# The compression of the sparse attention writes to PSUM banks 4 and 5 instead of 0 and 1

## The chip, the cores and the metric

The kernel runs on one core of a Trainium2 chip. The metric is the device time of one execution in microseconds (us), the median over the runs shown. Traces come from a profiled execution of the same program.

## The reference, cut to what matters

The kernel takes x (512 positions by 1024 channels, fp32) through four layers. The first two (a block with dilated attention and a gated convolution, then one with retention, each with a conv-GLU feed-forward) lie ahead of the place that the change touches. The last two are alike: a hybrid mixer and a feed-forward, each with a norm before and after. The mixer's input projection gives, among others, queries for 8 sparse-attention heads and keys and values for 2 KV heads in three kinds: compressed, selected, windowed. The part that matters here is the compression:

```
blocks = k[:, idx] + pe                      # 31 blocks of 32 positions, stride 16
flat   = blocks as rows of 32*64
kc, vc = gelu(flat @ w1 + b1) @ w2           # for keys (i = 0) and values (i = 1)
```

The keys go through a rotary embedding first ("rope"), the values do not.

## The kernel before

**Layout.** Activations lie transposed: 128 channels on the partitions, 512 positions along the free dimension. Every fp32 matmul with a weight is made as three fp32r matmuls, high times high (L496), low weight times high (L499) and high times low (L503). ScalarE makes the high part of each weight piece from the ring of four 512 KB slots (L1016), VectorE the low part (L1397); SyncE loads the ring, one unit behind the other.

**PSUM banks.** There are eight. `next_bank()` deals them in rotation from a list, and one counter (`turn[1]`) runs through the whole program. In the input projection of a hybrid layer the list is `[0, 1, 4, 5, 6, 7]`; banks 2 and 3 serve the norm. `empty(b)` makes TensorE wait until the last reader of bank b has told its semaphore, as the table `vacated` has it.

**The order on TensorE in hybrid layer l (0 or 1).** Five tiles of the projection are made together (`group`, tiles g 0 to g 4, five banks of the rotation), then tiles 5, 6 and 7 one after the other (three more banks). Then comes the compression (L863 to L883): for i = 0 and 1 and two parts each, 16 x 2 matmuls of 64x64 weights with 32 columns (L879), 64 columns of one bank for each i. It waits for the rope of tile g 0 (i = 0) or for tile g 1 read out (i = 1), for the bank, and for each raw weight unit. Behind it comes `by_token(("tm", l))` (L573, L574, L577): four banks, 0 to 3, in turn, 8 weight pieces, 280 columns; inside it, after the fourth piece, the second matmuls of the compression (`compressed`, L893 and L897), into banks 4, 5 and 6.

**The readers.** VectorE reads the eight tiles of the projection out, times the norm's row (`times_rs`, L1447), in the order g 0, g 1, g 2, and then, for r = 2 to 6:

```
        for r in range(2, 7):
            key = ("n", l, "g", r + 1) if r < 4 else ("n", l, r + 1)
            lo_for(("n", l, 5))
            rope(r - 2)
            lo_for(("n", l, 6))
            q.wait_ge(F.dve, ("rope", l, r - 2))
            times_rs(K.tmp(2 * r % 4), key, s, ("ra", l, r))
```

So tile 5 is read out only after `rope(2)`, tile 6 after `rope(3)` and tile 7 after `rope(4)`. A rope swaps halves by four small DMAs (`half_turn`, L431, on SyncE's queue, among the loads of the ring, L453), multiplies the swapped copy on VectorE (L1839) and the straight one on GpSimd (L2054), and adds the two (L1842). The swap of rope(r) starts when its tile has been read out; the copies share two buffers by turns.

ScalarE copies the compression's bank to SBUF (`hb`, L1298), VectorE adds the parts up (L1862 to L1865) behind its last `times_rs`, and ScalarE makes the gelu (L1302). Between the two i, ScalarE and VectorE make the first three `tm` weight pieces; they lie behind `hb(0)` and behind VectorE's sums for i = 0 in their engines' order.

Of the kernel before, what the change touches and what calls it, by code (L numbers as in the profile page):

```python
# [13 lines left out]
ACT = mybir.ActivationFunctionType  # L14
# [376 lines left out]
def build(nc, D, out):  # L391
    with ExitStack() as ctx:
        K = memory(nc, ctx)
        K.D, K.out, K.W = D, out, weights(D)
        for program in (sync_program, scalar_program, vector_program, gpsimd_program, tensor_program):
            program(Count(), Queue(None), K)
        for flag in K.F:
            flag.count = 0
        block = ctx.enter_context(nc.Block())

        @block.sync
        def _(e):
            sync_program(e, Queue(e), K)

        @block.scalar
        def _(e):
            scalar_program(e, Queue(e), K)

        @block.vector
        def _(e):  # L410
            vector_program(e, Queue(e), K)

        @block.gpsimd
        def _(e):
            gpsimd_program(e, Queue(e), K)

        @block.tensor
        def _(e):
            tensor_program(e, Queue(e), K)
# [49 lines left out]
def tensor_program(e, q, K):  # L469
    F, W, BK = K.F, K.W, K.BK  # L470
    vacated = {}
# [3 lines left out]
    def empty(b):  # L475
        for flag, event in vacated.get(b, ()):
            q.wait_ge(flag, event)
# [248 lines left out]
    for i in range(NQ):  # L726
        m = e.transpose(BK[4][0:48, i * 128:(i + 1) * 128], K.HL[:, 48 * i:48 * i + 48].bitcast(F32), K.cs("ident"))
# [4 lines left out]
    for n, j in enumerate((0, 4, 1, 5, 2, 6, 3, 7)):  # L732
# [6 lines left out]
        m = e.matmul(BK[b][:, :], K.wh(p, c * 128, 128), K.RT, start=True, stop=True)  # L739
# [71 lines left out]
    for h in range(4):  # L811
        for kt in range(NQ):
            w = S - kt * 128
            empty(kt)
            for part in range(2):
                for which in range(2):
                    q.wait_ge(F.pool, ("rot", h, which, part))
                m = e.matmul(BK[kt][:, 0:w], K.RQ[2 + part][:, kt * 128:(kt + 1) * 128], K.RQ[part][:, kt * 128:S],
                             start=part == 0, stop=part == 1)
# [4 lines left out]
        for m_ in range(4):  # L824
            empty(m_)
            for kt in range(NQ):
                q.wait_ge(F.dve, ("wt", h, kt))
                q.wait_ge(F.dve, ("rvc", h, kt))
                m = e.matmul(BK[m_][:, kt * 128:S], K.RV[:, kt * S + m_ * 128:kt * S + (m_ + 1) * 128],  # L829
                             K.WT[kt][:, 0:S - kt * 128], start=kt == 0, stop=kt == 3, skip_group_check=True)  # L830
# [25 lines left out]
    for l in range(2):  # L856
# [8 lines left out]
        for i in range(2):  # L865
            c = (K.kcr, K.vcr)[i]
            if i == 0:
                q.wait_ge(F.dve, ("rope", l, 0))
            else:
                q.wait_ge(F.dve, ("freed", "n", l, "g", 1))  # L870
            q.wait_ge(F.dve, ("pe", l))
            empty(i)
            for part in range(2):
                u = W.raws["w1", l, 2 * i + part]
                q.wait_ge(K.landed(u), ("unit", u))
                for n in range(16):
                    for kv in range(2):
                        r = slice(64 * kv, 64 * kv + 64)
                        m = e.matmul(BK[i][r, 32 * part:32 * part + 32], K.slot(u)[r, n * 64:(n + 1) * 64],  # L879
                                     c[r, 2 * part:2 * part + 32, n], start=part == 0 and n == 0, stop=n == 15,  # L880
                                     skip_group_check=True)
                m.then_inc(F.attn.tell(("cmp", l, i, part), ("unit", u)), 1)
            vacated[i] = [(F.act, ("hb", l, i))]  # L883

        def compressed():

# [17 lines left out]
        for g in range(4):  # L904
# [4 lines left out]
            for i in range(NQ):  # L909
                c0 = (g % 2 * 4 + i) * 64  # L910
                m = e.matmul(BK[b][:, c0:c0 + 64], K.NQT[g][:, i * 128:(i + 1) * 128], K.kcc, start=True, stop=True,
                             skip_group_check=True)
# [87 lines left out]
def scalar_program(e, q, K):  # L1000
    F, W, BK = K.F, K.W, K.BK
    nxt = [0]

    def hi_to(p):

        while nxt[0] <= min(p, len(W.pieces) - 1):
            i = nxt[0]
            nxt[0] += 1
            u, c, w = W.pieces[i]
            if i == 0:  # L1010
                q.wait_ge(F.first, "first")
            else:
                q.wait_ge(K.landed(u), ("unit", u))
            if i >= SPLIT:
                q.wait_ge(F.proj, ("piece", i - SPLIT))
            e.activation(K.wh(i, 0, w), K.raw(i), ACT.Copy, bias=0.0, scale=1.0).then_inc(F.hi.tell(("piece", i)), 1)  # L1016
# [271 lines left out]
    for l in range(2):  # L1288
# [6 lines left out]
            hi_for(("n", l, i))  # L1295
        for i in range(2):
            q.wait_ge(F.attn, ("cmp", l, i, 1))
            e.activation(K.hb(i), BK[i][:, 0:64], ACT.Copy, bias=0.0, scale=1.0).then_inc(F.act.tell(("hb", l, i)), 1)  # L1298
            if i == 0:
                hi_to(W.first["tm", l] + 2)  # L1300
            q.wait_ge(F.dve, ("hid", l, i))
            e.activation(K.hid[:, 64 + 32 * i:95 + 32 * i], K.hid[:, 32 * i:32 * i + 31], ACT.Gelu_apprx_tanh,  # L1302
                         bias=K.SM[:, 160 + i:161 + i], scale=1.0).then_inc(F.act.tell(("gel", l, i)), 1)
# [32 lines left out]
        for t in range(18):  # L1336
            pair = (2 * t, 2 * t + 1)
            kt = 3 - t % 4
            if t < 16:
                if t and (t - 1) % 4 < 3:  # L1340
                    for n in (2 * t - 2, 2 * t - 1):
                        m, kt1 = n // 8 * 2 + n % 2, 3 - n % 8 // 2
# [895 lines left out]
```

## Time and profile before

| what | value |
|---|---|
| runs before (us) | 3029.17, 3024.3, 3022.35; median 3024.3 |
| the profiled execution's own time | 3025.72 us |
| its span | 3024.0 us |
| mean granted TensorE clock | 0.994 |
| TensorE busy | 2997.6 us (99%) |
| VectorE, ScalarE, GpSimd busy | 1770.5, 1268.6, 151.0 us |

The busy time of an engine is that of its instructions; a granted clock of 1.00 is 2.4 GHz, 0.50 is 1.2 GHz. A timeline row has the start, the time taken, the engine, the line, and in brackets the idle time ahead with the work that ended it. PEld is TensorE's weight load.

### The profile page before, as it was taken

The numbers are of one execution on the slowest core, as the hardware profiler recorded it, in microseconds if no ns is written. First come the engines' busy times: TensorE is split into PE (matmuls) and PEld (weight loads), VectorE is DVE, ScalarE is ACT, GpSimd is POOL, SyncE is SP. The second block draws the span as 40 slices with busy tenths as digits, with TensorE's granted clock in tenths as the row PEclk, the third lists the DMA queues.
The fourth block names the chain that finished last, engine by engine and source line by source line (L and its number), as shares of the span: only waits on it lengthen the run. The fifth ranks groups of instructions, "written<-read, shape, count | busy, mean of one in ns | idle before, by whom it ended". The sixth has DMA issues, their size and how long they took to land.

```text
span 3024.0 us, 37960 instructions
## 1 busy us (share of the span) xinstructions
PE 2997.6 (99%) x14676; PEld 2403.7 (79%) x14676; DVE 1770.5 (59%) x3129; ACT 1268.6 (42%) x2377; POOL 151.0 (5%) x203
## 2 busy tenths in 40 slices
PE   9999999999999999999999999999999999999998
PEld 7778888878888888888876687888887766888887
DVE  4666775345555587634565558774455655587743
ACT  4444443322333344432366535443233655354431
POOL 0100000000000000001001101000020011010000
PEclk9999999999999999999999999999989999999999
DMA  4222322222222333334201132322242111223332
GB/s 150 76 98 91 102 96 96 97 77 84 84 77 85 97 98 98 98 96 133 91 29 49 42 98 84 105 97 95 80 125 90 33 46 46 94 85 104 98 98 70
DMA packets 74724, 263.97 MB, mean 87 GB/s; under 512 B 9008, under 2 KB 9008, under 8 KB 74416
## 3 DMA queue, kind: packets, MB, share of 16 engines
q1 hardware_dynamic: 73680, 258.13, 26.4%
q10 hardware_dynamic: 864, 3.41, 0.3%
q8 instruction: 116, 1.90, 0.3%
q14 instruction: 64, 0.52, 0.1%
HBM read 255.74 MB, written 2.10 MB: 85 GB/s over the span
## 4 chain that ended last, share of the span: by engine, by line
PE 89%; DVE 7%; ACT 2%; issue 1%; DMA 1%; POOL 0%; SPq 0%; DVEq 0%; POOLq 0%; ACTq 0%
PE bank L496 24%; PE bank L503 23%; PE bank L499 23%; PE bank L573 2%; PE bank L577 2%; PE bank L574 2%; PE bank L661 2%; PE bank L693 2%; PE bank L675 1%; DVE wl L1397 1%; PE bank L829 1%; PE bank L930 1%; DVE x L1821 1%; DVE big L1981 1%; PE bank L960 1%
## 5 line engine op out<-in xcount | busy, mean ns | idle before, releaser
L1397 DVE TENSOR_TENSOR wl<-ring,wh 128x512 fp32r<-128x512 f32 (+1 forms) x946 | 650.8, 694 | 824.9 <-ACT wh L1016 819.9
L496 PE MATMUL bank<-xh,wh 128*128 128x512 f32 x2464 | 982.1, 399 | 3.3 <-ACT xh L1023 2.6
L499 PE MATMUL bank<-xh,wl 128*128 128x512 f32 x2464 | 961.9, 390 | 2.3 <-DVE wl L1397 2.3
L503 PE MATMUL bank<-xl,wh 128*128 128x512 f32 x2464 | 924.0, 390 | 0.0
L1016 ACT ACTIVATE wh<-ring 128x512 fp32r<-128x512 f32 (+1 forms) x946 | 580.4, 622 | 788.6 <-PE bank L503 706.0
L496 PEld LDWEIGHTS bank<-xh,wh 128*128 128x128 f32 x2464 | 463.5, 188 | 137.3 <-issue 37.0
L503 PEld LDWEIGHTS bank<-xl,wh 128*128 128x128 f32 x2464 | 463.0, 188 | 98.6 <-DVE xl L1490 0.4
L499 PEld LDWEIGHTS bank<-xh,wl 128*128 128x128 f32 x2464 | 463.7, 188 | 93.3 <-DVE wl L1397 4.8
L496 PE MATMUL bank<-bigr,wh 128*128 128x512 f32 x1024 | 399.0, 390 | 0.5 <-ACT bigr L1380 0.5
L499 PE MATMUL bank<-bigr,wl 128*128 128x512 f32 x1024 | 398.4, 389 | 0.0
L503 PE MATMUL bank<-bigr,wh 128*128 128x512 f32 x1024 | 393.4, 389 | 0.0
L496 PEld LDWEIGHTS bank<-bigr,wh 128*128 128x128 f32 x1024 | 192.2, 188 | 41.3 <-ACT bigr L1380 1.4
L503 PEld LDWEIGHTS bank<-bigr,wh 128*128 128x128 f32 x1024 | 192.2, 188 | 40.8 <-DVE bigr L1985 0.9
L499 PEld LDWEIGHTS bank<-bigr,wl 128*128 128x128 f32 x1024 | 192.2, 188 | 39.7
L1193 ACT ACTIVATE tmp<-tmp,vec 128x512 f32<-128x512 f32 x136 | 104.7, 770 | 182.0 <-DVE tmp L1447 182.0
L1085 ACT ACTIVATE pp<-pp,sm 128x512 f32<-128x512 f32 (+3 forms) x160 | 88.3, 553 | 90.6 <-DVE sm L1466 90.5
L1203 ACT ACTIVATE bigr<-tmp 128x512 fp32r<-128x512 f32 x88 | 55.6, 632 | 138.3 <-DVE tmp L1654 138.3
L2010 POOL TENSOR_TENSOR sm<-sm,cst 128x4 f32<-128x4 f32 x16 | 16.6, 1037 | 1936.1 <-DVE sm L1419 1601.9
L1447 DVE TENSOR_TENSOR big<-bank,rs 128x512 f32<-128x512 f32 x106 | 71.6, 687 | 68.6 <-PE bank L503 65.4
L1447 DVE TENSOR_TENSOR tmp<-bank,rs 128x512 f32<-128x512 f32 x154 | 105.3, 684 | 6.0 <-ACT rs L1031 4.3
L573 PE MATMUL bank<-wh,xh 128*128 128x512 f32 (+1 forms) x288 | 107.9, 375 | 0.0
L577 PE MATMUL bank<-wl,xh 128*128 128x512 f32 (+1 forms) x288 | 106.7, 370 | 0.1
(204 smaller groups left out, 2777.6 us busy)
## 6 DMA issues: line engine op xcount, KB each, us to landing
ring<-in_w_up SPq DMA_DIRECT2D x176, 512.0 KB, 3.4
ring<-in_w_down SPq DMA_DIRECT2D x88, 512.0 KB, 3.4
ring<-in_w_in SPq DMA_DIRECT2D x64, 512.0 KB, 3.5
ring<-in_w_ret SPq DMA_DIRECT2D x32, 512.0 KB, 3.2
ring<-in_w_even SPq DMA_DIRECT2D x19, 512.0 KB, 3.3
ring<-in_w_ret_v SPq DMA_DIRECT2D x16, 512.0 KB, 3.2
ring<-in_w_ret_out SPq DMA_DIRECT2D x16, 512.0 KB, 3.3
ring<-in_w_proj SPq DMA_DIRECT2D x16, 512.0 KB, 3.5
```

Of the source, the lines that this page charges most:

```text
L496: e.matmul(o, K.wh(p, c * 128, 128), oh, start=start, stop=False, skip_group_check=True)
L499: e.matmul(o, K.wl(p, c * 128, 128), oh, start=False, stop=False, skip_group_check=True)
L503: m = e.matmul(o, K.wh(p, c * 128, 128), ol, start=False, stop=stop, skip_group_check=True)
L573: e.matmul(o, K.XH[:, c], K.wh(p, 0, n), start=k == 0, stop=False)
L574: e.matmul(o, K.XL[:, c], K.wh(p, 0, n), start=False, stop=False)
L577: m = e.matmul(o, K.XH[:, c], K.wl(p, 0, n), start=False, stop=k == DT - 1)
L661: m = e.matmul(BK[i][:, u.at:u.at + w], u.q[r, u.qt * 128:w], u.k[r, 0:w], start=True, stop=True, skip_group_check=True)
L1016: e.activation(K.wh(i, 0, w), K.raw(i), ACT.Copy, bias=0.0, scale=1.0).then_inc(F.hi.tell(("piece", i)), 1)
L1085: e.activation(p, p, ACT.Exp, bias=K.den(t, 2 * part + i, 0), scale=-1.0, accum_out=K.den(t, 2 * part + i, 1)).then_inc(F.act.tell(("exp", ...
L1193: e.activation(K.tmp((2 * i + 1) % 5), K.up(i), ACT.Identity, bias=b, scale=w[2]).then_inc(F.act.tell(("tap", f, i)), 1)
L1397: e.tensor_tensor(K.wl(i, 0, w), K.raw(i), K.wh(i, 0, w).bitcast(F32), ALU.subtract).then_inc(F.lo.tell(("piece", i)), 1)
L1447: e.tensor_tensor(dst, K.bank(key)[:, :], K.RSB[:, :], ALU.mult).then_inc(F.dve.tell(("freed", *key), *events), 1)
```

## The change

The compression writes to banks 4 + i instead of i, it waits for those banks to be empty, `vacated` has the entry for them, and ScalarE's copy reads from them. Nothing else differs.

```diff
@@ -869,18 +869,18 @@
             q.wait_ge(F.dve, ("pe", l))
-            empty(i)
+            empty(4 + i)
             for part in range(2):
                 u = W.raws["w1", l, 2 * i + part]
                 q.wait_ge(K.landed(u), ("unit", u))
                 for n in range(16):
                     for kv in range(2):
                         r = slice(64 * kv, 64 * kv + 64)
-                        m = e.matmul(BK[i][r, 32 * part:32 * part + 32], K.slot(u)[r, n * 64:(n + 1) * 64],
+                        m = e.matmul(BK[4 + i][r, 32 * part:32 * part + 32], K.slot(u)[r, n * 64:(n + 1) * 64],
                                      c[r, 2 * part:2 * part + 32, n], start=part == 0 and n == 0, stop=n == 15,
                                      skip_group_check=True)
                 m.then_inc(F.attn.tell(("cmp", l, i, part), ("unit", u)), 1)
-            vacated[i] = [(F.act, ("hb", l, i))]
+            vacated[4 + i] = [(F.act, ("hb", l, i))]
@@ -1295,7 +1295,7 @@
             q.wait_ge(F.attn, ("cmp", l, i, 1))
-            e.activation(K.hb(i), BK[i][:, 0:64], ACT.Copy, bias=0.0, scale=1.0).then_inc(F.act.tell(("hb", l, i)), 1)
+            e.activation(K.hb(i), BK[4 + i][:, 0:64], ACT.Copy, bias=0.0, scale=1.0).then_inc(F.act.tell(("hb", l, i)), 1)
```

## Rows read from the trace of the kernel before

**Rows 1.** The page: engines busy, and the chain that ended last by engine.

```profile
PE 2997.6 (99%) x14676; PEld 2403.7 (79%) x14676; DVE 1770.5 (59%) x3129; ACT 1268.6 (42%) x2377; POOL 151.0 (5%) x203
PE 89%; DVE 7%; ACT 2%; issue 1%; DMA 1%; POOL 0%; SPq 0%; DVEq 0%; POOLq 0%; ACTq 0%
```

**Rows 2.** Timeline of TensorE, layer 1: last projection matmul, compression, by-token matmuls.

```profile
2231.62 0.39 PE L503 MATMUL bank<-xl,wh 128*128 128x512 f32 x1
2235.46 4.78 PE L879 MATMUL bank<-big,ring 64*64 64x32 f32 x97 [3.45 <-DVE tmp L1447]
...
2248.67 0.60 PE L573 MATMUL bank<-wh,xh 128*128 128x280 f32 x1
...
2249.30 0.43 PE L577 MATMUL bank<-wl,xh 128*128 128x280 f32 x1
2249.53 0.43 PE L573 MATMUL bank<-wh,xh 128*128 128x280 f32 x1
```

**Rows 3.** Timeline of VectorE, layer 1: tiles 5 and 7 read out, and what follows.

```profile
2234.67 0.69 DVE L1447 TENSOR_TENSOR tmp<-bank,rs 128x512 f32<-128x512 f32 x1
...
2240.19 0.69 DVE L1839 TENSOR_TENSOR pp<-pp,rope 128x512 f32<-128x512 f32 x1 [1.25 <-DMA pp<-tmp]
...
2242.84 0.69 DVE L1447 TENSOR_TENSOR tmp<-bank,rs 128x512 f32<-128x512 f32 x1
...
2243.81 1.17 DVE L1397 TENSOR_TENSOR wl<-ring,wh 128x280 fp32r<-128x280 f32 x3
```

**Rows 4.** Timeline of SyncE's DMA issues, layer 1: two swaps and the loads behind.

```profile
2231.29 2.40 SPq L431 DMA_DIRECT2D pp<-tmp  x4
...
2235.39 3.37 SPq L431 DMA_DIRECT2D pp<-tmp  x4
2238.80 6.88 SPq L453 DMA_DIRECT2D ring<-in_w_tm  x3
```

**Rows 5.** Stretches, layers 1 and 0: length, busy PE, PEld, DVE, ACT, POOL, clock, DMA.

```profile
2236.00:2236.50 0.50, 0.50 (x20) 0.50 (x18) 0.29 (x1) 0.00 (x0) 0.50 (x1) 0.72 0.90 369
...
2244.00:2249.00 5.00, 5.00 (x90) 4.93 (x89) 0.97 (x3) 0.47 (x2) 0.00 (x0) 0.50 0.47 136
...
2253.00:2253.50 0.50, 0.50 (x5) 0.50 (x4) 0.50 (x1) 0.00 (x0) 0.50 (x1) 0.72 1.02 418
...
1413.00:1417.00 4.00, 4.00 (x132) 3.79 (x130) 1.02 (x3) 0.00 (x0) 1.71 (x1) 1.00 0.70 198
```

**Rows 6.** Timeline of TensorE, layer 0: compression, then by-token matmuls.

```profile
1413.22 7.66 PE L879 MATMUL bank<-big,ring 64*64 64x32 f32 x256
1420.81 0.40 PE L573 MATMUL bank<-wh,xh 128*128 128x280 f32 x1
...
1422.02 0.29 PE L574 MATMUL bank<-wh,xl 128*128 128x280 f32 x1
1422.15 0.29 PE L577 MATMUL bank<-wl,xh 128*128 128x280 f32 x1
```

**Rows 7.** Timeline of VectorE, layer 0: tiles 5 and 6 read out.

```profile
1412.44 0.69 DVE L1447 TENSOR_TENSOR tmp<-bank,rs 128x512 f32<-128x512 f32 x1
...
1417.53 0.69 DVE L1447 TENSOR_TENSOR tmp<-bank,rs 128x512 f32<-128x512 f32 x1
```

**Rows 8.** Timeline of ScalarE, layer 0: the compression's banks copied out.

```profile
1417.19 0.22 ACT L1298 ACTIVATE big<-bank 128x64 f32<-128x64 f32 x1 [14.11 <-PE bank L879]
...
1421.54 0.20 ACT L1298 ACTIVATE big<-bank 128x64 f32<-128x64 f32 x1
```

**Rows 9.** Timeline of the weight loads, layer 0: what the by-token matmuls waited for.

```profile
1421.40 0.19 PEld L577 LDWEIGHTS bank<-wl,xh 128*128 128x128 f32 x1 [0.30 <-DVE wl L1397]
1421.79 0.19 PEld L573 LDWEIGHTS bank<-wh,xh 128*128 128x128 f32 x1 [0.20 <-ACT big L1298]
```

**Rows 10.** An idle stretch of over 1 us elsewhere: timeline, and the stretch around it.

```profile
95.24 0.50 PE L739 MATMUL bank<-bigr,wh 128*128 128x512 f32 x1 [1.18 <-DVE big L1557]
...
95.00:100.00 5.00, 4.11 (x10) 1.70 (x11) 5.00 (x9) 1.09 (x1) 0.00 (x0) 1.00 0.32 105
```

## The prediction

> **What bounds the kernel.** I read the page first: TensorE is busy for 2997.6 of 3024.0 us and carries 89% of the chain that ended last [rows 1]. A microsecond in which TensorE stands still in the middle is thus a microsecond of the total, unless a later wait on something other than TensorE takes it up. Next I read the timeline of TensorE around line 879, once in each hybrid layer. In layer 1 the projection ends at 2231.62 + 0.39 = 2232.01 and the compression starts at 2235.46, after an idle stretch of 3.45 us; it is let go by a VectorE read-out [rows 2]. That is the one starting 2234.67 and ending 2235.36 [rows 3]. In layer 0 there is no such gap [rows 6]. Then the stretches: in layer 1 the granted clock falls to half during the half microsecond from 2236.0 and comes back in the one from 2253.0; in layer 0 it stays 1.00 [rows 5]. 256 matmul records of compression thus take 2248.67 - 2235.46 = 13.21 us in layer 1 [rows 2] and 1420.81 - 1413.22 = 7.59 us in layer 0 [rows 6].
>
> **Who held the banks.** The question is who was last in banks 4 and 5. The counter of the rotation has to be counted in the code. Ahead of layer 0 it has dealt 5 + 12 + 8 banks in the first block, 52 in each feed-forward (5 + 39 + 8) and 16 + 12 + 8 in the retention: 25 + 52 + 36 + 52 = 165, which is 3 modulo 6. Layer 0 therefore gives tiles g 0 to g 4 the banks 5, 6, 7, 0, 1 and tiles 5, 6, 7 the banks 4, 5, 6. One layer deals 8 + 8 + 16 + 4 + 16 + 8 + 52 = 112, 4 modulo 6. Layer 1 starts one place in: g 0 to g 4 in 1, 4, 5, 6, 7, and tiles 5, 6, 7 in 0, 1, 4. The trace bears this out: in layer 1 bank 0 would be freed by tile 5, the read-out at 2234.67, and that is the one TensorE waited for. So the new waits are: layer 0, i = 0 for tile 5 and i = 1 for tile 6; layer 1, i = 0 for tile 7, and i = 1 for tile g 2, long read out.
>
> **The change, layer 1.** Tile 7's read-out starts at 2242.84 and ends at 2243.53 [rows 3]; TensorE followed such an end by 0.10 us (2235.46 against 2235.36), so the compression starts at 2243.63. Is that end itself moved? It hangs on rope(4): tile 5 read out at 2235.36, its swap issued at 2235.39 [rows 4], landed for VectorE's multiply at 2240.19, then GpSimd's product, the sum, and the read-out at 2242.84 [rows 3]. No step waits for the compression; the ring load queued behind the swap on SyncE (2238.80) waits for it, the swap does not [rows 4]. At best the swap gains from there being no `tm` load beside it and issues in 2.40 us like the one before, instead of 3.37 [rows 4]: 0.97 us sooner. At worst nothing is gained. I take nothing, because the `tm` load starts only after the swap's last issue, and keep 1.0 us for the range. **Start: + 2243.63 - 2235.46 = + 8.17 us**, idle 3.45 + 8.17 = 11.6 us.
>
> How fast does it then run? Before, the first 0.76 us ran at the full clock (2235.46 to about 2236.22, from the mean of 0.72 in its half microsecond) and did 0.76 / 7.59 x 256 = 26 records; the other 230 took 12.45 us. All 256 at half clock are 12.45 x 256 / 230 = 13.86 us. The clock fell 4.2 us after the last projection matmul; 11.6 us of idling holds that, so all of it runs at half. **+ 0.65 us.** The clock did not come back in 12.45 us of compression, but 2253.3 - 2248.67 = 4.6 us into the by-token matmuls; I take the same again (0). The bound there: a by-token matmul takes its turn every 0.13 us at the full clock [rows 6] and every 0.23 us at half clock [rows 2], so if the clock rose 2 us sooner or later it moves the time by about 1 us either way.
>
> The records have 32 columns. The Trainium skill ("TensorE: Matmul & The Clock Gate", section "Wait — 56ns, not 53.3ns?") states a floor of about 25 ns start to start however few the columns, and columns over 1.2 GHz when cold, 26.7 ns here: by it the compression would take as long at one clock as at the other, and the 0.65 would be nothing, the sum 8.9. The rows speak against it for this pair of small weight load and matmul: 7.59 / 256 = 30 ns and 13.86 / 256 = 54 ns. The rows decide.
>
> **The change, layer 0.** For i = 0, tile 5 is read out at 1412.44 + 0.69 = 1413.13 [rows 7], plus 0.10 is 1413.23, and the compression started at 1413.22 [rows 6]: 0, at most 0.1. For i = 1, the first half ends near 1417.02 (ScalarE's copy starts at 1417.19 [rows 8], half of 7.59 us past the start is 1417.02). Tile 6 is read out at 1417.53 + 0.69 = 1418.22 [rows 7], start 1418.32: TensorE stands 1.30 us. What is taken away: by_token waited 0.30 us for the low piece, and then 0.20 us for `hb(1)` ahead of its second bank [rows 9]. Its first matmul starts at 1420.81 [rows 6], its fourth at 1421.79 [rows 9]. Now the first starts at 1422.11. The low piece was ready by 1421.40 (the L577 start [rows 9]), hb(1) is no longer asked for, so the fourth follows after 0.23 (the step behind a restart, 1421.79 to 1422.02) + 0.13 + 0.13 (the step after it [rows 6]) = 0.49 us, at 1422.60. **+ 0.81 us.** What loses its cover: ScalarE's copy of i = 1 moves from 1421.54 to about 1422.2, and with it gelu and weight pieces 3 and 4; TensorE needs piece 3 only after 36 matmuls of 0.13 us, at 1426.8, so nothing shows. The third `tm` load waits for the first part of i = 1 and comes 1.3 us later, for pieces 6 and 7; also covered. VectorE queues nothing new behind TensorE: in layer 0 its wait for hb(0) ends as before.
>
> In layer 1 the loads of all three `tm` units, ScalarE's copies and VectorE's sums slide by the same 8.2 us as TensorE, with the same leads or, at half clock, longer ones: 0.
>
> **Sum.** 8.17 + 0.65 + 0.81 = 9.6 us. Nothing behind takes it up: TensorE is idle for 3024.0 - 2997.6 = 26.4 us in all [rows 1], of which 3.45 is the wait that grows here, and no load runs short that a pause would let catch up. Against the profiled execution (3025.72, span 3024.0) it gives 3035.3; against the median of the runs shown, 1.4 below it, 3033.9. I give 3034.
>
> **Rivals.**
> 1. *The clock also falls in layer 0.* The new 1.3 us idle lies in the midst of the sparse compression matmuls. For it: in layer 1 the clock fell after 3.45 us of idling although the compression had been running again for 0.76 us, so such work counts for little. Against: 7.6 us of it kept the clock in layer 0 [rows 5], and an idle of 1.18 us elsewhere left the clock up, though it lay among dense work [rows 10]. Price: up to 3.8 us of compression at 54 instead of 30 ns, 3.1 us, and 4.6 us of by-token matmuls at 0.23 instead of 0.13 us, 2.0 us; from half of each to all of it 2.6 to 5.1 more, 3036.6 to 3039.1. The Trainium skill, same page, section "A second HAM failure mode: psum-queue depth-cycling", says that brief idles between groups while banks are cycled make the clock go to and fro; it would bring this rival about, and no row decides it. Chance 0.2.
> 2. *Not slower: bank 4 is free early in layer 1.* If my count is off and bank 4 was last a g tile, the wait of 3.45 us goes instead of growing. It decides at 2232.01: a holder read out by then costs nothing. TensorE then starts at 2232.1 and finishes at the full clock at 2239.7, but by_token needs the low piece that VectorE makes at 2243.81, behind tile 7's read-out [rows 3]; it starts near 2244.3 in place of 2248.67, 4.4 us sooner, and 2 more if the clock holds. With layer 0's 0.8 that is 3020.7, down to 3018.7. Against it: the count, and that the wait in the trace fits it. Chance 0.04.
> 3. *Most of it is not seen.* The fall of the clock in layer 1 of the profiled execution was close (a gap of 3.45 us). Should the other executions of before differ from it, or the swap go much faster unhindered, the difference is smaller: start + 7.2, rise of the clock 2 us sooner, 1 us off; with layer 0 it is about 7, and with the spread of the runs (3022.35 to 3029.17) it may read below 6. About 3030. Chance 0.12. If on the contrary some executions of before kept the clock, theirs lay lower and the new one always pays: that end is 3039 to 3040.
>
> **How the numbers follow.** Forecast 0.64, rivals 0.2, 0.04, 0.12. The range runs from 3030 (rival 3, the 1.0 us of the swap, the spread of the runs) to 3040 (rival 1 at its dearest). About 0.2%, 6 us, is what a measurement of this kernel can tell from no change: forecast and rival 1 lie beyond it, rival 3 within it, rival 2 within or below. Faster 0.03, same 0.12, slower 0.85.
>
> **What would show it.** In layer 1, idle before line 879 of some 11.6 us ended by the VectorE read-out that follows the last rope; a granted clock of 0.50 that starts in that idle stretch and lasts till 4 or 5 us into the by-token matmuls, and 13.9 us of compression. In layer 0, an idle of 1.3 us in mid-compression, the L577 and L573 waits gone, and 1.00 throughout. Wrong would be: a wait ended by another tile's read-out, no idle in layer 1, or a later stage in which TensorE waits less than before.

## The result, and the profile after

| | before | changed |
|---|---|---|
| median of 7 runs each (us) | 3024.73 | 3032.05 |
| lowest to highest | 3022.35 to 3029.17 | 3029.9 to 3037.51 |
| span of the profiled execution | 3024.0 | 3029.6 |
| its own time | 3025.72 | 3031.38 |

The ratio is 1.0027, with a 95% interval from 1.0016 to 1.0039: 7.3 us slower by the medians, where 9.6 were forecast. A second set of runs, made later (below), gave 3034.52 against 3025.88, a ratio of 1.0025 (1.0015 to 1.0034).

Timeline of TensorE in the changed kernel, layer 1, the rows that answer to [rows 2]:

```profile
2230.29 0.39 PE L503 MATMUL bank<-xl,wh 128*128 128x512 f32 x1
2241.32 13.86 PE L879 MATMUL bank<-big,ring 64*64 64x32 f32 x256 [10.64 <-DVE tmp L1447]
2255.11 0.60 PE L573 MATMUL bank<-wh,xh 128*128 128x280 f32 x1
```

The idle stretch has grown from 3.45 to 10.64 us, and it is again a VectorE read-out that ends it. Which one shows in VectorE's timeline of the same stretch, which answers to [rows 3]:

```profile
2233.33 0.69 DVE L1447 TENSOR_TENSOR tmp<-bank,rs 128x512 f32<-128x512 f32 x1
...
2236.65 0.69 DVE L1447 TENSOR_TENSOR tmp<-bank,rs 128x512 f32<-128x512 f32 x1
2237.88 0.69 DVE L1839 TENSOR_TENSOR pp<-pp,rope 128x512 f32<-128x512 f32 x1 [0.54 <-DMA pp<-tmp]
2239.80 0.69 DVE L1842 TENSOR_TENSOR big<-tmp,pp 128x512 f32<-128x512 f32 x1 [1.22 <-POOL tmp L2054]
2240.52 0.69 DVE L1447 TENSOR_TENSOR tmp<-bank,rs 128x512 f32<-128x512 f32 x1
```

The three read-outs are those of tiles 5, 6 and 7. The last ends at 2241.21 and TensorE follows at 2241.32: bank 4 was tile 7's. It starts 7.19 us behind tile 5's here, and 8.17 before. The difference begins in the swap of the last rope. From its first issue on SyncE's queue (SPq) to the multiply on VectorE that waits for it, it took 3.83 us here (2234.05 to 2237.88) and 4.80 before; the four issues took 2.41 us, and 3.37 in [rows 4]:

```profile
2234.05 2.41 SPq L431 DMA_DIRECT2D pp<-tmp  x4
2244.97 7.16 SPq L453 DMA_DIRECT2D ring<-in_w_tm  x3
```

The stretches (columns as in [rows 5]: length, busy time of PE, PEld, DVE, ACT and POOL, granted clock, DMA share, GB/s):

```profile
2231.00:2234.00 3.00, 0.00 (x0) 0.00 (x0) 1.75 (x3) 0.00 (x0) 1.50 (x1) 1.00 0.78 261
2234.00:2241.00 7.00, 0.00 (x0) 0.00 (x0) 3.94 (x7) 0.00 (x0) 3.40 (x2) 0.50 0.30 97
2241.00:2255.00 14.00, 13.69 (x256) 13.72 (x256) 1.71 (x7) 1.41 (x5) 0.00 (x0) 0.50 0.33 98
2255.00:2257.50 2.50, 2.50 (x14) 2.44 (x13) 1.55 (x7) 0.87 (x3) 1.28 (x1) 0.50 0.43 105
2257.50:2258.50 1.00, 1.00 (x8) 1.00 (x7) 0.23 (x1) 0.29 (x1) 0.00 (x0) 0.79 0.33 70
1411.00:1419.00 8.00, 7.94 (x258) 7.62 (x256) 3.95 (x7) 1.54 (x5) 3.42 (x2) 1.00 0.68 219
```

The clock falls in the idle stretch, stays at half through the whole compression (2241.32 to 2255.11, 13.79 us) and rises about 2.8 us into the by-token matmuls (a mean of 0.79 in the microsecond from 2257.5 puts it near 2257.9). In layer 0 it stays up. Layer 0 on TensorE, first its weight loads and then its matmuls, to be read with [rows 6] and [rows 9]:

```profile
1411.20 3.83 PEld L879 LDWEIGHTS bank<-big,ring 64*64 64x64 f32 x128 [0.35 <-DVE tmp L1447]
1415.21 3.81 PEld L879 LDWEIGHTS bank<-big,ring 64*64 64x64 f32 x128 [0.18 <-DVE tmp L1447]
1420.09 0.19 PEld L577 LDWEIGHTS bank<-wl,xh 128*128 128x128 f32 x1 [0.73 <-DVE wl L1397]
```

```profile
1411.22 7.92 PE L879 MATMUL bank<-big,ring 64*64 64x32 f32 x256
1419.07 0.40 PE L573 MATMUL bank<-wh,xh 128*128 128x280 f32 x1
1419.30 0.29 PE L574 MATMUL bank<-wh,xl 128*128 128x280 f32 x1
1420.09 0.40 PE L577 MATMUL bank<-wl,xh 128*128 128x280 f32 x1 [0.50 <-DVE wl L1397]
1420.33 0.29 PE L573 MATMUL bank<-wh,xh 128*128 128x280 f32 x1
```

There is a pause between the halves, but a small one: compression start to by-token start is 7.85 us against 7.59. The wait for `hb(1)` is gone. The one for the low piece has grown from 0.30 to 0.73 us.

**Where the 5.6 us of the spans come from.** The changed execution reached layer 0's compression 2.0 us sooner (1411.22 against 1413.22), long before anything that the change touches. The timed runs of one kernel spread by as much. So I compare distances within one execution, from a matmul ahead of the change to one behind it. From the start of layer 0's compression to the feed-forward's matmul at 1815.35 before, 1813.98 after: 402.13 and 402.76 us, so layer 0 costs 0.6. From layer 1's last projection matmul to the one at 2644.97 before, 2650.58 after: 413.35 and 420.29, so layer 1 costs 6.9. Together 7.6, less the 2.0 of the start.

### The profile page after: what moved, and what is told of

The parts are those of the page before. It is cut to its first block, busy times and chain, and to the rows that moved or that the text cites. A ratio compares the mean times of both kernels' runs of the same rounds, so it can differ in the third digit from the quotient of the medians.

```text
span 3029.6 us, 37956 instructions
## 1 busy us (share of the span) xinstructions
PE 2995.4 (99%) x14676; PEld 2402.9 (79%) x14676; DVE 1769.0 (58%) x3129; ACT 1268.2 (42%) x2377; POOL 151.7 (5%) x203
## 4 chain that ended last, share of the span: by engine, by line
PE 89%; DVE 7%; ACT 2%; issue 1%; DMA 1%; POOL 0%; SPq 0%; DVEq 0%; POOLq 0%; ACTq 0%
PE bank L496 24%; PE bank L499 23%; PE bank L503 23%; PE bank L573 2%; PE bank L577 2%; PE bank L574 2%; PE bank L661 2%; PE bank L693 2%; PE bank L675 1%; DVE wl L1397 1%; PE bank L829 1%; PE bank L930 1%; DVE x L1821 1%; DVE big L1981 1%; PE bank L960 1%
```

## The experiments

Three questions: is it layer 1's wait for tile 7 and nothing else; what part is the clock; what does another bank give. The time of before differs a little from one set of runs to the next, so each kernel is given with its ratio to the runs of before of the same set, and the microseconds over or under before come from that ratio. A distance in layer 1 is that from its last projection matmul to the feed-forward's, as above: 413.35 us in the first profile of before, 413.48 in the second.

### One layer at a time

Diff for `l0_only`, against before (`l1_only` has the two cases the other way round):

```diff
-            empty(i)
+            empty(i if l else 4 + i)
```

and likewise in the matmul, in `vacated` and in ScalarE's copy.

> Banks 4 and 5 in hybrid layer 0 alone; layer 1 keeps banks 0 and 1. Theory (the loss is layer 1's wait for tile 7): TensorE pauses 0.2 to 1.3 us in mid-compression of layer 0 and gets about 0.5 back behind it, so 0.3 to 0.8 us over before, and the clock stays at full there. Rival A (the clock is upset in layer 0 too): 2.6 to 5 us over before and a granted clock of 0.50 from about 1417. Layer 1 as before: idle of 3.4 us ahead of line 879.

> Banks 4 and 5 in hybrid layer 1 alone; layer 0 keeps 0 and 1. Theory: the idle stretch ahead of line 879 in layer 1 is 10.6 to 11.6 us, ended by the third of VectorE's last read-outs, 7.2 to 8.2 more than before; the compression takes 13.8 us at half clock; in all 6.5 to 8.8 us over before, with layer 0 as before. Rival A puts 2 to 4 us of the loss in layer 0: then this one is 3 to 5 over before.

Measured: `l0_only` 3026.2 us, ratio 1.0004 (0.9995 to 1.0014); `l1_only` 3033.32 us, ratio 1.0025 (1.0015 to 1.0036), that is 7.6 us. The loss sits in layer 1. In its profile:

```profile
2244.17 13.87 PE L879 MATMUL bank<-big,ring 64*64 64x32 f32 x256 [10.66 <-DVE tmp L1447]
```

and in that of `l0_only`, where layer 1 is as before:

```profile
2236.66 13.87 PE L879 MATMUL bank<-big,ring 64*64 64x32 f32 x256 [3.45 <-DVE tmp L1447]
```

Layer 0's share, the same distance as above, is 403.10 us in `l0_only` and 402.21 in `l1_only`: 0.9. Rival A, the clock upset in layer 0, did not occur: in the profile of `l0_only` the clock stayed at 1.00 there.

### The two banks swapped

Against the changed kernel:

```diff
-            empty(4 + i)
+            empty(5 - i)
```

and likewise in the other three places.

> Bank 5 for i = 0 and bank 4 for i = 1 in both layers. Theory (the read-out of the tile that held the bank sets the start): in layer 1 the first half starts at once in bank 5 (tile g 2, long read out), runs 3.8 us, and the second half waits some 6.5 to 7 us for tile 7 in bank 4; the compression as a whole ends 6 to 7 us sooner than in the changed kernel, within 1.5 us of before. In layer 0 the first half waits for tile 6, 4 to 5 us of idling that the kernel before doesn't have, and the second half finds bank 4 free. If such an idle stretch puts the clock to half, as it did in layer 1, the compression of layer 0 takes 10 to 14 us instead of 7.6. Total 7 to 14 us over before. Rival (banks 4 and 5 cost something whoever held them): layer 1 as in the changed kernel.

Measured: 3037.73 us, ratio 1.0036 (1.0023 to 1.0048), 10.9 us over before. TensorE's timeline, layer 0 and then layer 1:

```profile
1417.75 13.87 PE L879 MATMUL bank<-big,ring 64*64 64x32 f32 x256 [4.16 <-DVE tmp L1447]
1431.55 0.60 PE L573 MATMUL bank<-wh,xh 128*128 128x280 f32 x1
...
2244.13 3.93 PE L879 MATMUL bank<-big,ring 64*64 64x32 f32 x128
2254.89 7.04 PE L879 MATMUL bank<-big,ring 64*64 64x32 f32 x128 [6.83 <-DVE tmp L1447]
2261.85 0.60 PE L573 MATMUL bank<-wh,xh 128*128 128x280 f32 x1
```

In layer 1 the first half runs at once, at the full clock, in bank 5; only the second waits, for the read-out at 2254.14 + 0.69 = 2254.83, the third behind the projection. Last projection matmul to by-token start is 18.0 us, against 24.8 in the changed kernel and 17.1 in the first profile of before. So what decides the wait is who was in the bank, not which bank it is. In layer 0 a bank that the kernel before found free now costs 4.16 us of idling, and the clock falls with it: the compression takes 13.80 us in place of 7.59. Nothing in layer 0 but that wait changed, so 6.2 us of clock came with 4.2 us of idling. With the by-token matmuls at half clock behind it, layer 0's distance from its last projection matmul to the feed-forward's is 414.31 us in place of 402.45.

### Filling the idle time

First with 46 dummy matmuls ahead of the compression of layer 1, in the changed kernel (`keep(n, b)` makes n matmuls of 512 columns into bank b, whose results nobody reads):

```diff
+        if l:
+            keep(46, 5)
         for i in range(2):
```

> The changed kernel with 46 dummy matmuls of 512 columns (about 9.9 us of work) into bank 5 ahead of the compression of layer 1, in the time in which TensorE idles. They keep the clock up and free nothing. Theory (idle time and clock add up): the compression still starts after tile 7's read-out, takes 7.6 instead of 13.8 us, and the by-token matmuls gain 1.2: 7.4 us under the changed kernel, thus about level with before (within 1.5 us). Rival C (the half clock costs this compression next to nothing, as its 32 columns are held by a floor per matmul): the changed kernel's time less 1.2 at most.

Measured: 3032.7 us, ratio 1.0029 (1.0017 to 1.0041): nothing gained over the changed kernel (1.0027). The theory, about level with before, missed, and the stretches of this profile say why (columns as above; two of layer 0, three of layer 1):

```profile
1410.00:1416.00 6.00, 5.55 (x184) 5.32 (x180) 2.77 (x4) 0.22 (x1) 2.35 (x2) 1.00 0.52 164
1417.00:1423.00 6.00, 6.00 (x62) 5.93 (x61) 3.93 (x15) 3.77 (x9) 1.36 (x2) 0.50 0.56 162
2231.00:2242.00 11.00, 11.00 (x51) 9.04 (x49) 4.97 (x8) 0.00 (x0) 5.20 (x3) 1.00 0.51 150
2243.40:2246.00 2.60, 2.60 (x90) 2.60 (x91) 0.00 (x0) 0.00 (x0) 0.00 (x0) 1.00 0.00 0
2246.50:2255.00 8.50, 8.50 (x162) 8.44 (x159) 1.59 (x6) 1.52 (x5) 0.00 (x0) 0.50 0.53 159
```

The clock stayed up as long as the fillers ran. Then came 1.04 us of idling and the compression, and 2.7 us into it the clock fell, though PE reads fully busy. Layer 1's distance is 419.87 us, 0.4 less than in the changed kernel. The clock fell in layer 0 too, where no filler was added, from before 1417. There the weight loads waited 0.16 us for tile 6 at the middle of the compression and, 15 loads further on, 0.52 us more (0.40 between the matmuls), which the trace puts down to no other engine ("issue"). It cost layer 0 3.4 us. That is rival 1 of the prediction, in this one of the five profiles with banks 4 and 5 in that order in layer 0; the longer of its two pauses is no wait for a bank.

So dense matmuls were strewn into the compression as well:

```diff
+        if l:
+            keep(46, 7)
...
                 m.then_inc(F.attn.tell(("cmp", l, i, part), ("unit", u)), 1)
+                if l and (i, part) != (1, 1):
+                    keep(3, 7)
```

> The changed kernel with 46 dummy matmuls ahead of the compression of layer 1 and 3 behind each of its first three parts. The first try had only the 46, and the clock fell within the compression. Theory (dense matmuls strewn among the parts hold it): the compression starts as in the changed kernel, takes 7.6 + 2.8 us at full clock, and the by-token matmuls gain about 1: 3.4 for the compression and 1 for these, thus 4 to 5 us under the changed kernel and 2 to 4 over before. If the clock falls all the same: 2 us over the changed kernel.

Measured: six timed runs in two groups, 3027.76 and 3029.57, then 3035.68 to 3041.75; the ratio of 1.0028 (1.0014 to 1.0042) is over both. The profiled execution was of the upper group, and its clock had fallen by the second part:

```profile
2242.50:2244.50 2.00, 1.93 (x64) 1.93 (x64) 0.02 (x1) 0.00 (x0) 0.00 (x0) 1.00 0.00 0
2245.00:2260.00 15.00, 15.00 (x202) 12.66 (x201) 1.50 (x6) 1.52 (x6) 0.89 (x1) 0.50 0.36 105
```

The lower group lies where an upheld clock was expected, 2 to 4 us over before. Its mean clock over the whole execution is the higher one too, 0.997 and 0.998 against 0.993 to 0.995, but no profile fell on such a run, so where in it the clock was up is not shown. The same treatment of the kernel before, `keep(14, 7)` and three times `keep(3, 7)`:

> The kernel before with dummy matmuls of 512 columns in layer 1: 14 ahead of the compression, in the idle time, and 3 behind each of its first three parts. Theory (the compression's small matmuls alone don't hold the clock, dense ones strewn among them do): the compression starts as before, takes 7.6 + 2.0 us at full clock, and the by-token matmuls run at the full clock: 4.5 to 5.6 us under before. Rival (the fall came from the idle stretch's place in time alone and comes all the same): a granted clock of 0.50 in the stretch, and up to 2 us over before from the fillers.

Measured: 3021.68 us, ratio 0.9983 (0.9974 to 0.9992), 5.1 us under before, although it does 23 matmuls more. The stretch over the whole of it:

```profile
2232.00:2248.00 16.00, 15.76 (x291) 13.32 (x290) 8.31 (x21) 2.09 (x8) 5.16 (x3) 1.00 0.65 192
```

Clock 1.00 throughout; last projection matmul to by-token start 14.5 us in place of 17.1. In `before_warm` the pause behind the fillers was 0.24 us, in `after_warm2` 1.26. The 5.1 us are what is left after the fillers' own cost: from the start of the compression to that of the by-token matmuls it is 10.65 us here and 7.59 in layer 0, so the nine fillers among the parts take 3.1. The half clock by itself therefore costs the kernel before some 8 us, by this estimate. For the changed kernel only the lower group of `after_warm2` speaks: 5 to 7 us under the 3034.52 of the changed kernel in the same set.

### Banks outside the rotation

Against before:

```diff
-            empty(i)
+            empty(2 + i)
```

and likewise in the other three places.

> The compression goes to banks 2 and 3, which the rotation doesn't hold and which the norm has long left. Theory: in layer 1 TensorE starts the compression at once, 3.45 us sooner than before, the clock stays up through it (7.6 us), and then the by-token matmuls wait some 4 us for the low piece that VectorE makes behind tile 7's read-out; they start 4.4 us sooner than before; layer 0 gains up to 0.5. So 4.4 to 7 us under before, about 3019. Rival B (the projection stage is held by the chain of ropes on VectorE whatever the bank): the by-token matmuls start as before and the time stays within 1 us of before.

Measured: 3021.6 us, ratio 0.9985 (0.9976 to 0.9994), 4.5 us under before. TensorE's timeline, layer 1:

```profile
2227.93 0.39 PE L503 MATMUL bank<-xl,wh 128*128 128x512 f32 x1
2228.25 5.79 PE L879 MATMUL bank<-big,ring 64*64 64x32 f32 x192
2234.46 2.06 PE L879 MATMUL bank<-big,ring 64*64 64x32 f32 x64 [0.42 <-DMA ring<-in_w]
2239.36 0.60 PE L573 MATMUL bank<-wh,xh 128*128 128x280 f32 x1 [2.84 <-ACT wh L1016]
...
2240.86 0.60 PE L577 MATMUL bank<-wl,xh 128*128 128x280 f32 x1 [0.66 <-DVE wl L1397]
```

The compression starts at once and runs at the full clock, as expected. New waits come up in turn: the last raw weight unit, then the high piece (its load stands behind the last swap on SyncE), then the low piece (behind tile 7's read-out on VectorE). The second of them, 2.84 us, I had not foreseen; it was hidden under the low piece's in my reckoning. The clock fell in that pause and came back 6.6 us into the by-token matmuls. They start 5.6 us sooner than before, and layer 1's distance is 409.19 us, 4.2 less.

The last wait can be taken away by letting VectorE do the sums for i = 0 and the first three low pieces ahead of the last rope:

```diff
             lo_for(("n", l, 5))
+            if r == 6:
+                part_sums(0)
             rope(r - 2)
...
-        for i in range(2):
-            hb, bias = K.hb(i), K.SM[:, 160 + i:161 + i]
...
+        part_sums(1)
```

with banks 2 and 3; `part_sums(i)` is the body of the old loop.

> Banks 2 and 3, and VectorE makes the sums of i = 0 and the first three low pieces ahead of the last rope. Theory: the by-token matmuls of layer 1 no longer wait for the low piece (0.66 us with banks 2 and 3) and in layer 0 0.3 us less; what is left is the wait for the high piece, that is for the ring load behind the last swap on SyncE. 1 us under the kernel with banks 2 and 3, 4 to 6 under before.

> As early_sums, with 10 dummy matmuls (2.2 us) between the compression and the by-token matmuls of layer 1, in the idle time of 2.8 us that banks 2 and 3 showed there. Theory: the clock stays up; the by-token matmuls gain 3 us where the clock fell otherwise, nothing where it stayed: 6 to 8.5 us under before. Rival (the clock falls during the compression itself): no gain over early_sums.

Measured: `early_sums` 3018.22 us, ratio 0.9972 (0.9961 to 0.9982), 8.5 us under before. `early_sums_warm`, the same with `keep(10, 7)` behind layer 1's compression, 3018.09 us, ratio 0.9973 (0.9962 to 0.9984): no difference. These two are the fastest of all kernels run here. TensorE's timeline of `early_sums`, layer 1:

```profile
2236.99 2.78 PE L879 MATMUL bank<-big,ring 64*64 64x32 f32 x64 [1.03 <-DMA ring<-in_w]
2240.46 0.60 PE L573 MATMUL bank<-wh,xh 128*128 128x280 f32 x1 [0.70 <-ACT wh L1016]
```

The lead of `early_sums` over `banks23` is 4.0 us by the ratios, whose intervals overlap, where 1 was expected. Layer 1's distance is 407.08 us, 2.1 less than with banks 2 and 3 alone, and layer 0's is 0.6 less; the rest stays open. The rival, a fall of the clock within the compression, did occur in this profile: its last 64 matmuls, behind 1.03 us of idling, take 2.78 us in place of 2.06, and the clock is back 4.4 us into the by-token matmuls. In the profile of `early_sums_warm`, where only 0.25 us of idling lay ahead of those 64, the clock stayed up throughout. Its by-token matmuls started 0.8 us later (11.6 us behind the projection, against 10.9), but layer 1's distance is 406.09 us, 1.0 less than in `early_sums`. That the timed runs show no such gain is no surprise, as they spread by 4.7 to 6.5 us in either kernel; whether there is one, they don't show.

### Both kernels once more

> The kernel before once more, for a second profile. Open is the term of the swap of the last rope in layer 1, whose four issues took 3.37 us in the first profile of before and 2.41 in that of the changed kernel. If that was chance: 2.4 us here, and tile 7's read-out starts 7.2 us after tile 5's, not 8.2. If the compression running beside it slows the issues in the kernel before: 3.4 again. The idle stretch is 3.45 us either way, and the time that of before.

> The changed kernel once more, for a second profile and more timed runs. Idle ahead of line 879 in layer 1 of 10.6 us with a swap of 2.4 us, 11.6 with one of 3.4; half clock through all of the compression, 13.8 us; in layer 0 a net loss of 0.6 to 1.0 us. The ratio to before between 1.0020 and 1.0030.

Measured: before 3026.14 us, ratio 1.0000 (0.9991 to 1.0009), which tells how well this comparison can say "no change"; changed 3034.52 us, ratio 1.0025. SyncE's queue, first before and then changed:

```profile
2235.14 3.38 SPq L431 DMA_DIRECT2D pp<-tmp  x4
```

```profile
2233.16 2.41 SPq L431 DMA_DIRECT2D pp<-tmp  x4
```

The difference is no chance. From the swap's first issue to the multiply it is 3.83 us in all three profiles of the changed kernel and `l1_only`, and 4.80 and 4.81 in those of before. Tile 7's read-out starts this far behind tile 5's in layer 1:

| TensorE in that time | kernel: us |
|---|---|
| idle | changed 7.19, 7.18 (again); l1_only 7.19 |
| compression for 1.2 us, then idle | swapped 7.27 |
| compression | before 8.17, 8.18 (again); l0_only 8.04; banks23 8.40 (idle at the end) |
| dummy matmuls | after_warm 8.00; after_warm2 8.27 |
| compression and dummy matmuls | before_warm 8.18 |

The dummy matmuls put into the changed kernel are the experiment: same banks, same waits, the `tm` load behind the read-out as in the changed kernel, TensorE at work instead of idle, and the rope chain is 0.8 to 1.1 us slower (4.61 and 4.88 us from issue to multiply, in place of 3.83). By what way TensorE's work slows the swap was not settled: in `l0_only` the four issues took 2.41 us and the chain was slow nevertheless. Nor is it the whole of what moves such a swap. In layer 0 the swap of rope 3 took 4.6 to 4.8 us from issue to multiply in all five profiles with banks 4 and 5 in that order, 5.0 in `swapped`, where TensorE stood idle behind the projection, and 5.8 to 6.5 in the seven that leave layer 0 as it was or use banks 2 and 3, with TensorE at work in all but `swapped`.

## Why the prediction was right, point by point

**Who held the banks: right.** The count of the rotation gave tiles 5 and 6 in layer 0, tile 7 and g 2 in layer 1; the read-outs that end the idle stretches, and the swapped kernel, bear it out.

**Start in layer 1, + 8.17 us: right in mechanism, too large.** It measured 10.64 - 3.45 = 7.19. The step that was off is "I take nothing, because the `tm` load starts only after the swap's last issue": the swap was 0.97 us faster, the end of the range that I had named. The reason given for that end, the missing `tm` load, was wrong: it is missing in `after_warm` and `after_warm2` too, and the chain is slow there. What goes with the quick swap is TensorE standing still.

**Compression at half clock, + 0.65: right.** 13.79 us in both profiles of the changed kernel, 13.86 forecast. Before took 13.21 in one profile and 13.80 in two (`before_again`, `l0_only`), so the term is 0 to 0.6, and that it was forecast as 0.65 hung on the one profile that was at hand. By an estimate from the floor that the Trainium skill states in "TensorE: Matmul & The Clock Gate", section "Wait — 56ns, not 53.3ns?", about the same time was due at both clocks (25 and 26.7 ns a matmul); the swapped kernel's layer 0, 13.80 against 7.59 with the same instructions, shows that it does not hold for this pair of load and matmul. The sum without the term would have been 8.17 + 0.81 = 9.0, not 8.9 as the prediction has it.

**Rise of the clock, 0 taken: within its bound.** It rose 2.8 us into the by-token matmuls in the first profile of changed, after 4.6 in the first of before, and 5.4 us in the second, after 3.2 in the second of before. At 0.13 against 0.23 us a matmul that is - 0.8 us for the first pair and + 1.0 for the second.

**Layer 0, + 0.81: right in size by luck, wrong in its parts.** 0.6, 0.9 and 1.0 us were measured (changed, l0_only, changed again). The pause of 1.30 us was 0.26: the swap of rope 3 was quicker, and tile 6's read-out came 4.0 us behind tile 5's in place of 5.1 (3.8 to 4.0 in all five profiles with this order of banks, 5.0 to 5.8 in the seven that leave layer 0 as it was or use banks 2 and 3). So it goes with the choice of banks and is no chance; why, no run here tells. "The low piece was ready by 1421.40" failed as well, the other way: tile 7's read-out fell 8.19 us behind tile 5's in place of 7.50, and the wait for the low piece grew from 0.30 to 0.73 us. Two errors, 1.0 us too much and 0.4 too little, left the size near.

**The sum.** 7.19 + 0.58 - 0.8 + 0.6 = 7.6 for the first pair of profiles, against 9.6. For the second pair it is 7.18 + 0 + 1.0 + 1.0 = 9.2; the distances give 8.0 in layer 1 and 1.0 in layer 0, 9.0 in all. The timed medians say 7.3 for the first set and 8.6 for the second (7.6 by its ratio). The mechanism is the one forecast, and the size 0.6 to 2.3 us too large, of which the swap is 1.0.

**Rivals.** 1, the clock in layer 0: did not happen in the profiles of the change itself, but in one of the five with that order of banks. The section cited for it, "A second HAM failure mode: psum-queue depth-cycling" in the same page of the Trainium skill, tells of short idles behind which the clock goes to and fro. Here it fell once, behind pauses of which the longer is no wait for a bank, so this case neither bears the section out nor speaks against it. 2, not slower: fell with the count. Its reckoning of what a free bank gives, 4.4 us, was met by `banks23` with 4.5, in part by luck: the by-token matmuls start 5.6 us sooner, and a later rise of the clock and a further wait of 0.66 us take some of it back. 3, most of it not seen: the difference was seen, but its terms (start + 7.2, a clock that rises 2 us sooner, layer 0, about 7 in all) are those of the first pair of profiles, and the 7.3 of the medians lies nearer to them than to 9.6.

## What to carry to other kernels

A bank of a rotation is as free as its last reader is early. Before work is moved to another bank, count the dealing through to that place in every pass of the loop; here the two passes come out at different places of the same list, and the pass with the late reader sets the price. An idle stretch of TensorE ahead of a run of small matmuls can be paid twice: in `swapped` 4.2 us of idling brought 6.2 us of half clock in its wake. And a gain from fillers is net of their own time: about 8 us of half clock, 3.1 us of fillers, 5.1 us won.

## What had not been expected

- The clock can fall in the midst of back-to-back matmuls: in `after_warm` it fell 2.7 us into the compression of layer 1, behind 1.04 us of idling, and in `early_sums` 1.0 us into matmuls behind 1.03 us of idling. 46 dense matmuls ahead of that idling did not prevent it in `after_warm`. In layer 0 of before the same 256 matmuls kept it, with no such pause ahead. Three dense matmuls between each part kept it in `before_warm` (0.24 us of idling ahead), but not in the profile of `after_warm2` (1.26 us ahead).
- The half-swapping DMAs of the last rope in layer 1 are quicker while TensorE stands still: the read-out that hangs on them came 7.2 us behind the earlier one instead of 8.0 to 8.4.
- In layer 0 the swap of rope 3 lands 1.0 us or more sooner when the compression goes to banks 4 and 5, in all five such profiles. The cause is open.
